# First layer's attention: the order of ScalarE's copies and exponentials, and of each tile's end, and a projection that starts on its first four rows

## What is computed

```
logits = einsum(q, k_sel) * HD**-0.5 + bias       # keys outside the top k: -1e30
probs  = softmax(logits)
y_b    = einsum(probs, v_sel)
x      = x + concat([y_a, y_b], -1) @ w_out_even   # 1024 x 1024
```

## Time and profile before

| | |
|---|---|
| median of 3 runs | 1670.54 us (1670.27 to 1670.81) |
| profiled execution, own time | 1668.23 us |
| profiled execution, span from first to last instruction | 1666.4 us |
| TensorE busy in the span | 1601.7 us, 96% |
| VectorE, ScalarE, GpSimd busy | 986.6, 633.8, 634.6 us |
| mean granted TensorE clock | 0.984 of full speed |

### The profile page before, as it was taken

One profiled execution on the slowest core, in us unless ns is written; L12 is line 12 of the kernel. 1 busy time (PEld: TensorE's weight loads), 2 busy tenths in 40 slices (PEclk: granted clock), 3 DMA queues, 4 the chain that ended last, 5 costly groups with the idle time before them and its releaser, 6 DMA issues.

```text
span 1666.4 us, 31076 instructions
## 1 busy us (share of the span) xinstructions
PE 1601.7 (96%) x11914; PEld 1512.0 (91%) x11914; DVE 986.6 (59%) x1413; ACT 633.8 (38%) x959; POOL 634.6 (38%) x305
## 2 busy tenths in 40 slices
PE   8999888998999999999999979999899999999999
PEld 7889744996899999999999979799699999999999
DVE  7699964566356555455656879465645554045530
ACT  6333364335333332233334655433534333123320
POOL 3345520431134444333435645633023444334442
PEclk9999998999999999999999989999999999999999
DMA  5342320242032232222222322324012223222232
GB/s 190 117 146 94 119 75 1 88 136 80 26 114 77 87 102 87 76 88 88 97 84 93 115 70 89 127 89 167 23 52 88 88 87 101 77 78 86 88 105 89
DMA packets 41859, 153.53 MB, mean 92 GB/s; under 512 B 5489, under 2 KB 6129, under 8 KB 40505
## 3 DMA queue, kind: packets, MB, share of 16 engines
q1 hardware_dynamic: 41784, 152.49, 27.3%
HBM read 145.27 MB, written 9.30 MB: 93 GB/s over the span
## 4 chain that ended last, share of the span: by engine, by line
PE 72%; issue 13%; POOL 8%; DVE 3%; ACT 3%; DMA 1%; POOLq 0%; SPq 0%; DVEq 0%; ACTq 0%
PE PS L857 64%; POOL WLO L419 8%; PE AX L1166 2%; DVE RSTD L1281 1%; PE AX L1076 1%; PE AX L1104 1%; PE AX L1172 1%; DVE SQA L1327 1%; PE PS L1087 1%; ACT LG L652 1%; PE AX L924 0%; ACT WHI L450 0%; PE PS L1138 0%; DVE SQA L1304 0%; PE PS L1135 0%
## 5 line engine op out<-in xcount | busy, mean ns | idle before, releaser
L419 POOL TENSOR_TENSOR WLO<-WRAW,WHI 128x1024 fp32r<-128x1024 f32 (+3 forms) x301 | 634.4, 2117 | 1016.4 <-ACT WHI L450 1016.1
L450 ACT ACTIVATE WHI<-WRAW 128x1024 fp32r<-128x1024 f32 (+3 forms) x301 | 268.9, 914 | 675.8 <-PE PS L857 619.6
L857 PE MATMUL PS<-XH,WHI 128*128 128x272 f32 (+1 forms) x2240 | 470.1, 291 | 15.4 <-POOL WLO L419 9.0
L857 PE MATMUL PS<-XH,WLO 128*128 128x272 f32 (+1 forms) x2240 | 464.6, 289 | 0.0
L857 PE MATMUL PS<-XL,WHI 128*128 128x272 f32 (+1 forms) x2240 | 462.3, 288 | 0.0
L857 PEld LDWEIGHTS PS<-XH,WHI 128*128 128x128 f32 x2240 | 356.7, 189 | 24.3 <-POOL WLO L419 11.8
L857 PEld LDWEIGHTS PS<-XL,WHI 128*128 128x128 f32 x2240 | 356.3, 189 | 0.0
L857 PEld LDWEIGHTS PS<-XH,WLO 128*128 128x128 f32 x2240 | 354.3, 189 | 0.0
L857 PE MATMUL PS<-HH,WHI 128*128 128x272 f32 x1216 | 253.3, 290 | 0.7 <-DVE HL L1531 0.7
L857 PE MATMUL PS<-HL,WHI 128*128 128x272 f32 x1216 | 252.2, 289 | 0.0
L857 PE MATMUL PS<-HH,WLO 128*128 128x272 f32 x1216 | 252.1, 288 | 0.0
(11 more groups left out here) (259 smaller groups left out, 1664.8 us busy)
## 6 DMA issues: line engine op xcount, KB each, us to landing
WRAW<-in_w_in_even SPq DMA_DIRECT2D x29, 512.0 KB, 3.5
WRAW<-in_w_up0a SPq DMA_DIRECT2D x22, 512.0 KB, 3.4
WRAW<-in_w_up0b SPq DMA_DIRECT2D x22, 512.0 KB, 3.4
WRAW<-in_w_up1a SPq DMA_DIRECT2D x22, 512.0 KB, 3.5
WRAW<-in_w_up1b SPq DMA_DIRECT2D x22, 512.0 KB, 3.4
WRAW<-in_w_mv SPq DMA_DIRECT2D x16, 512.0 KB, 3.5
WRAW<-in_w_xq SPq DMA_DIRECT2D x16, 512.0 KB, 3.4
WRAW<-in_w_xo SPq DMA_DIRECT2D x16, 512.0 KB, 3.5
```

The lines of the kernel that those rows point to most:

```text
L419: pool.tensor_tensor(WLO[parity][:, first:last], WRAW[parity][:, first:last], WHIf[parity][:, first:last], ALU.subtract).then_inc(lo_done, ...
L450: act.activation(WHI[parity][:, first:last], WRAW[parity][:, first:last], ACT.Copy).then_inc(hi_done, 2 // len(cuts))
L857: ins = pe.matmul(dst, w, x, start=first, stop=last)
```

## The change

ScalarE takes copies and exponentials in turn: copy of the first unit of pair p-2, exponential of the first unit of pair p, copy of the second, exponential of the second. A tile's high part is made at the beginning of ScalarE's turn. VectorE makes the tile's low part between the two logit passes of pair p and the normalisations of pair p-1. The projection waits ahead of row block k: for 4 of `yl_even` at blocks 0 to 3 of its first chunk, for all 9 at blocks 4 to 7.

```
             for p in range(PAIRS + 4):          # ScalarE
-                if p < PAIRS:
-                    for u in (2 * p, 2 * p + 1):
+                if p >= 7 and (p - 7) % 4 == 0:
+                    evict_o((p - 7) // 4)
+                for u in (2 * p, 2 * p + 1):
+                    if 2 <= p < PAIRS + 2:
+                        evict_pt(u - 4)
+                    if p < PAIRS:
                         j = UNITS[u][0]
                         nq, nk = QTILES[j][1], QTILES[j][3]
                         act.wait_ge(lg_ready, u + 1)
                         act.activation(logits(u)[0:nq, 0:nk], logits(u)[0:nq, 0:nk], ACT.Exp, scale=-1.0,
                                        bias=STAT[0:nq, 0, u:u + 1], accum_out=STAT[0:nq, 1, u:u + 1]).then_inc(exp_done, 1)
-                if 2 <= p < PAIRS + 2:
-                    evict_pt(2 * p - 4)
-                    evict_pt(2 * p - 3)
-                if p >= 7 and (p - 7) % 4 == 0:
-                    evict_o((p - 7) // 4)
...
             c0, t0 = C0["out_even"], T0["out_even"]          # TensorE
-            pe.wait_ge(yl_even, A_TILES + 5)
-            linear("out_even", KT, HH, HL, None, 0)
+            linear("out_even", KT, HH, HL, yl_even, [A_TILES] * 4 + [A_TILES + 5] * 4)
...
+                if p >= 7 and (p - 7) % 4 == 0:          # VectorE, between logit passes and normalisations
+                    j = (p - 7) // 4
+                    q0, nq = QTILES[j][0:2]
+                    dve.wait_ge(yh_even, A_TILES + j + 1)
+                    src = AX[:, 2 + j % 2, 0:512].rearrange("p (t q) -> p t q", t=4)[:, :, 0:nq]
+                    dve.tensor_tensor(HL[:, 4:8, q0:q0 + nq], src, HHf[:, 4:8, q0:q0 + nq], ALU.subtract).then_inc(yl_even, 1)
                 for u in (2 * p - 2, 2 * p - 1):
...
-                if p >= 7 and (p - 7) % 4 == 0:          # the same five lines, behind the normalisations
```

## The result

The changed kernel takes 1660.97 us, median of 7 runs (1659.8 to 1666.15), beside 1670.54 us before (7 runs, 1669.84 to 1671.1). The ratio is 0.9947 with a 95% interval of 0.9937 to 0.9957: 9.6 us less by the medians, 8.9 by the ratio. The prediction said 1660.2, with a range of 1656.3 to 1665.5. The profiled execution took 1659.88 us with a span of 1658.1, 8.3 us less than its counterpart.

The account below looks back on a forecast made before the run. TensorE, busy 1601.7 of 1666.4 us, was taken as the bound. Savings of 5.8 (waits), 3.0 (clock) and 1.5 us (attention's end) sum to 10.3, giving 1660.2 us from a median of 1670.54, range 1656.3 to 1665.5.

Parts of the forecast that it names:

- case A: The full sum of savings holds: 1660.2 us, own range 1658.9 to 1661.8; chance 0.43.
- Terms (1) and (2): Attention: transposes' waits for copies go (7.2 us), less 1.4 for low parts ahead of normalisations: 5.8 us saved.
- the second fall: TensorE's half-speed clock from 267.05 to 273.45 us, around the fourth tile's product; forecast to go.
- the six waits: TensorE's transposes waiting for ScalarE's copies out of PSUM, 6.5 us in all; forecast to go.
- Term (3): Half-speed clock at the fourth tile's product goes: 3.0 us saved, bounds 0 and 3.0.
- Term (4): Attention's end, last logits to projection: low part's wait 0.74, projection's wait 0.70, earlier copies 0.1; 1.5 us saved.
- Term (5): Half-speed clock at the projection's start stays, relative to it; some 2.5 us if gone; all savings carried to the end.
- B: Rival: the second low clock stays or comes elsewhere in the attention, costing 3.0 us: 1663.2 us; chance 0.27.
- C: Rival: neither later clock fall comes, saving 2.5 us more: 1657.7 us; chance 0.14.
- the third fall: TensorE's half-speed clock from 280.80 to 287.20 us, at the projection's start; forecast to stay relative to the projection.
- D: Rival: TensorE waits about as long for VectorE's normalisations as before for copies: 1667.5 to 1670 us; chance 0.11.
- E: Rival: slower, ScalarE's waiting copies hold exponentials and limit the some 18 pairs: 1674 us or more; chance 0.05.

Follow-up runs that it names:

- the alternation: Kernel before with only ScalarE's copies and exponentials taken in turn, the high part still last: 1667.51 us, ratio 0.9980.
- the tile's end: Kernel before with only the high part moved first on ScalarE and the low part ahead of VectorE's normalisations: 1665.78 us, ratio 0.9956.
- the table early: Changed kernel plus one tiny exponential before the attention, so ScalarE's table of exponentials loads early: 1661.96 us, ratio 0.9936.

## Why the prediction was right, step by step

**The total.** 10.3 us forecast, 8.3 in the profiled execution, 9.6 in the medians, 8.9 by the ratio; case A was nearest. That the medians come within 1 us of 1660.2 is in part luck: the waits brought less than forecast, and what came behind the projection's start, which the sum had put at nothing, went both ways. The projection's start was forecast at 271.4 and measured at 272.62, with the attention starting 0.4 us later (51.24 us of length, 50.4 forecast). The case's own range was summed wrongly: with bounds of 1.4 and 1.0 us it is 1658.8 to 1661.2.

**Terms (1) and (2), 5.8 us: right in what goes, 1.0 us too large, and wrongly divided.** From the first logits to the fourth tile's product the attention fell from 48.40 to 42.82 us, 5.6 us with the part of the second fall that lay ahead of the product (0.8, the prediction's estimate), so 4.8 for the waits. In parts: nothing up to the first tile's product, 11.95 us in both, though a wait of 0.30 us had gone, and the likely reason is the first fall, which came later and covered more of TensorE's work; the sum had left that fall as it was. Then 3.29 us in the stretch at granted 1.00, where the three printed waits (0.19, 1.60, 1.63) make 3.42. Then 2.29 us to the fourth tile's product, 1.5 without the 0.8. The leftovers were in part as worked out. Three waits for normalisations were forecast at the 32-row tile (1.0, 0.1 and 0.2 us); one came, of 0.88, and the other that is printed there, 0.34, is for a copy. What was put wrongly is who earns it. The prediction gave the six waits to the alternation and the tile's end only a cost of 1.4. In the stretch at granted 1.00 the alternation alone brings 1.37 us, and the tile's end 2.18 alone and 1.92 on top of it: with the high part last, VectorE's logit pass stays late and the waits are renamed.

**Term (3), 3.0 us: right.** The product took 3.59 us instead of 5.81, 2.2 as forecast, at granted 1.00. That it hangs on both edits was not said: each alone kept a half-speed stretch before and in that product. Why the fall goes with both stays open; the prediction chose between gone and staying by the waits ahead of it.

**Term (4), 1.5 us: right.** From the last logits to the projection 6.49 became 267.79 to 272.62, 4.83 us: 1.7. Of it 0.83 lie ahead of the last product (4.93 to 4.10 us) and come with the tile's end, which has them alone too, and not with the alternation. The 0.7 for the early start is confirmed by the gap that returns without it; in the times of the changed kernel it is below what the runs resolve.

**Term (5): wrong in two ways that nearly cancel.** The fall at the projection lasted 3.3 us and not as before: VectorE's reciprocal that follows the projection starts at 331.68 instead of 342.14, 10.5 us earlier, where the projection started 9.1 earlier, so 1.4 us more. And the claim that all is carried to the end is not so: from the projection's start to the end the changed kernel took 1385.5 us, the one before 1666.4 - 281.69 = 1384.7. The longer half-speed stretch in the cross-attention (10.2 us for 6.7) took back, by estimate, half of its 3.5. In sum: 9.5 of length, less 0.4 by which the attention began later, plus 1.4, less 1.7 makes 8.8, where the span fell by 8.3; the other 0.5 was not traced.

**The rivals.** B did not come: the wait at the 32-row tile stayed without a fall behind it. C came by half: the third fall stayed and lasted 3.3 us for 6.4. D is refuted for the whole change and is near what the alternation alone does (1667.51 us, waits of 8.0 for 10.9). E is refuted by 8 us of added copies that cost 0.5 us of waits and nothing in the larger tiles. What the Trainium skill says on this (TensorE: Matmul & The Clock Gate, Architectural detail), strict order on ScalarE and VectorE, the traces bear out: a low part that waited for its high part held VectorE's next logit pass (263.99 and 264.60 in the earlier trace rows).

## What to carry to other kernels

When engines run hand-written orders in lockstep, replay two turns of all of them with measured durations before moving anything; a printed wait names only the last releaser, and a second one can stand just behind it. Taking one away is then worth little (the first transposes' wait fell from 1.73 to 1.44 us with the table early) and both a lot (to 0.21). Before calling a surplus of two edits such a pair, compare them where the clock was the same: here the surplus was the clock's. In this kernel work that must end a tile belonged at the head of the next turn of an engine that would otherwise wait, and behind whatever the bound engine needs next. Where the bound is TensorE, look also at its clock in every stretch: here falls that moved were worth 1 to 3 us, some of them in stages that were not edited.

## What the runs showed of the hardware

A VectorE multiplication of 128x128 from and to SBUF with one per-partition factor took 0.29 us alone and 1.93 us when it started 0.50 us into a GpSimd subtraction of 2.35 us; VectorE's next instruction started in the same 0.01 us in which GpSimd's ended. With the subtraction elsewhere it took 0.29 us again. The Trainium skill (SBUF — State Buffer, SBUF: two separate sides) describes a port pair that VectorE's two-port modes and GpSimd lock for a whole instruction; the trace agrees, though no run here shows which mode the multiplication was in. The logit passes of VectorE, which read PSUM and one SBUF operand, ran beside the same subtraction in 0.28 to 0.29 us.

TensorE's clock fell to 1.2 GHz after waits of no more than 1.6 to 1.9 us among busy work, in the stretches looked at, and stayed there for 3.2 to 10.2 us while TensorE was busy all or most of that time. What places the later falls stays open: filling one wait of 1.29 us ahead of a fall left it, filling one of 1.59 us came with another gone, each in one profiled execution. A fall's price hangs on what it hits: the fourth tile's product, matmuls alone, took 5.81 us for 3.59, while the stretch of 6.8 us at the attention's start cost 1.7.
